# Two blocks' shift strips moved from the norm stage into the projection, with their stage weights loaded twice

## The reference

```python
sh, sc, gt = adaln(c, w_ada[l], b_ada[l])              # silu(c) @ w_ada + b_ada, in thirds
sh_c, sc_c, gt_c = adaln(c_ctx[None], w_ada[l], b_ada[l])
h_l = rmsnorm(x_l, norm_g[l]) * (1.0 + sc) + sh        # 512 x 2048
h_c = rmsnorm(x_c, norm_g[l]) * (1.0 + sc_c) + sh_c    # 256 x 2048
u_l = h_l @ w_in[l]                                    # the projection, 39 column tiles of 128
u_c = h_c @ w_in[l][:, OFF_KV:OFF_MLA_G]
```

## Time and profile before

| | |
|---|---|
| median of the runs | 901.35 us |
| the profiled execution: its own time | 901.99 us |
| its span, first to last instruction | 900.2 us |
| busy: PE, DVE, ACT, POOL | 98%, 77%, 47%, 22% |
| mean granted TensorE clock | 0.997 of full |
| stage A on PE | until 126.7 us |
| DMA queue of SP | 147.25 MB of 184.08 |

### The profile page before, as it was taken

How to read it: one execution, slowest core, us unless ns; L and a number is a source line. 1 busy time by engine, 2 the same in 40 slices (tenths; PEclk the granted TensorE clock), 3 DMA queues, 4 the chain that set the end, 5 groups by cost and what they waited for, 6 DMA issues and landing times.

```text
span 900.2 us, 12252 instructions
## 1 busy us (share of the span) xinstructions
PE 886.3 (98%) x4750; PEld 739.2 (82%) x4750; DVE 696.5 (77%) x860; ACT 426.2 (47%) x633; POOL 200.0 (22%) x167
## 2 busy tenths in 40 slices
PE   9999999999999999999999999999999999999996
PEld 5776688888888888888888888989898988888885
DVE  5555898789997699967787484778687787879796
ACT  4655467434335434333324332645454456645464
POOL 1222200310003100001002753100000200495641
PEclk9999999999999999999999999999999999999998
DMA  9999932235473453578874242865657535875754
GB/s 362 417 420 421 409 145 95 89 129 189 143 183 106 114 167 117 187 232 325 314 295 162 94 140 94 181 228 141 135 171 198 123 140 187 305 228 187 234 186 187
DMA packets 36885, 184.08 MB, mean 204 GB/s; under 512 B 4411, under 2 KB 5819, under 8 KB 26716
## 3 DMA queue, kind: packets, MB, share of 16 engines
q1 hardware_dynamic: 32528, 147.25, 44.4%
q0 software_dynamic: 3968, 35.65, 16.2%
q10 hardware_dynamic: 332, 0.40, 0.1%
HBM read 177.39 MB, written 37.75 MB: 239 GB/s over the span
## 4 chain that ended last, share of the span: by engine, by line
PE 90%; DMA 4%; DVE 3%; ACT 2%; issue 1%; SPq 0%; ACTq 0%; DVEq 0%
PE pp L2346 41%; PE pp L2376 17%; PE pp L2656 17%; PE pp L2261 4%; DMA ada_raw<-in_w_ada_dram 3%; PE pp L2237 3%; PE pp L2622 2%; PE pp L2267 1%; PE pp L2613 1%; PE pp L2614 1%; DMA ada_raw<-in_w_scale_dram 1%; DVE softmax_stats L1854 1%; DVE pt_lo L1869 0%; ACT U L1140 0%; PE pp L2445 0%
## 5 line engine op out<-in xcount | busy, mean ns | idle before, releaser
L2346 PE MATMUL pp<-h_hi,w_hi 128*128 128x512 f32 x544 | 213.0, 391 | 0.0
L2346 PE MATMUL pp<-h_hi,w_lo 128*128 128x512 f32 x544 | 211.8, 389 | 0.0
L2346 PE MATMUL pp<-h_lo,w_hi 128*128 128x512 f32 x544 | 211.8, 389 | 0.0
L1569 DVE TENSOR_TENSOR w_lo<-w_raw,w_hi 128x1024 fp32r<-128x1024 f32 x68 | 91.0, 1339 | 62.6 <-ACT w_hi L931 61.8
L931 ACT ACTIVATE w_hi<-w_raw 128x1024 fp32r<-128x1024 f32 x68 | 71.8, 1056 | 130.8 <-PE pp L2346 114.9
L2346 PEld LDWEIGHTS pp<-h_hi,w_lo 128*128 128x128 f32 x544 | 102.1, 188 | 21.5
L2346 PEld LDWEIGHTS pp<-h_hi,w_hi 128*128 128x128 f32 x544 | 102.2, 188 | 21.1 <-DVE w_lo L1569 0.3
L2346 PEld LDWEIGHTS pp<-h_lo,w_hi 128*128 128x128 f32 x544 | 102.2, 188 | 20.5
L2656 PE MATMUL pp<-wo_hi,side_hi 128*128 128x512 f32 x224 | 87.3, 390 | 0.1
L2656 PE MATMUL pp<-wo_hi,side_lo 128*128 128x512 f32 x224 | 87.2, 389 | 0.0
L2656 PE MATMUL pp<-wo_lo,side_hi 128*128 128x512 f32 x224 | 87.2, 389 | 0.0
(11 more groups left out here) (368 smaller groups left out, 1930.8 us busy)
## 6 DMA issues: line engine op xcount, KB each, us to landing
w_raw<-in_wb_dram SPq DMA_DIRECT2D x68, 512.0 KB, 3.8
ada_raw<-in_w_ada_dram SPq DMA_DIRECT2D x15, 2048.0 KB, 13.5
w_out_sums<-in_w_out_dram POOLq DMA_DIRECT2D x16, 1024.0 KB, 10.4
w_gate_raw<-in_w_gate_dram SPq DMA_DIRECT2D x16, 1024.0 KB, 7.4
wo_raw<-w_out_sums SPq DMA_DIRECT2D x16, 1024.0 KB, 5.0
wo_raw<-in_w_out_dram SPq DMA_DIRECT2D x12, 1024.0 KB, 5.0
wa_raw<-in_wa_dram SPq DMA_DIRECT2D x14, 288.0 KB, 8.3
UG<-in_xT_dram SPq DMA_DIRECT2D x7, 512.0 KB, 9.2
```

The costliest lines, as they stand in the source:

```text
L1569: eng.tensor_tensor(lane(wb_lo, n % KW), lane(wb_raw, n % KW), lane(wb_hi, n % 2), ALU.subtract).then_inc(wb_lo_done, 1)
L2346: mm = eng.matmul(ps[i][:], w, x, start=(kk == 0 and m == 0), stop=(kk == KT - 1 and m == 2))
```

## The change

The shifts of blocks 0 and 1 are no longer made in stage A. Their `w_ada` load becomes the seventeenth, `LATE = 16`, behind all others. `ada_vectors(LATE)` stands in the projection behind part 0 of chunk 0, its `combine` behind chunk 1, ACT's `late_shifts` in chunk 2. The projection takes its channel blocks in the order 2, 3, ..., 15, 0, 1 (`place_of`, `block_at`), so that the tokens of blocks 0 and 1, which need these shifts, are made last, in chunk 2. `wa_first` is gone: the two weight blocks are loaded a second time for `shifted(0)` and `shifted(1)`, which DVE does in chunk 2.

The sums over the partitions can then be made only behind chunk 3 (`shift_columns`), and ACT copies them out there. `ps[0]` and `ps[1]` of the stage are copied out without the bias; `first_shifts` adds it in place in chunk 4, and only then come the two `centre`s, once in chunk 1. The `neighbour_taps` of tiles 0 and 1 move from chunk 2 to chunks 5 and 6. The context's sum of squares, once behind the shift sums, stays in the stage.

```diff
-NEIGHBOURS = (2, 2, 8, 8, 10, 10, 18, 19, 26, 26, 30, 34)
+NEIGHBOURS = (5, 6, 8, 8, 10, 10, 18, 19, 26, 26, 30, 34)
-EARLY, LATE = 2, 13
+EARLY, LATE = 2, KT
+def block_at(p):
+    return (p + EARLY) % KT
...
@@ SP @@
             for j in range(2, KT):
-                if j == LATE:
-                    load_ada(LATE)
-                load_ada(block_of(j))
+                load_ada(j)
...
+            load_ada(LATE)
             eng.wait_ge(ada_mm, KT - 1)
             for n in range(KW):
                 load_b(n)
             load_decay(0)
             load_decay(1)
+            load_wa(KT)
             eng.wait_ge(scaled, 4)
             load_w3(0)
             eng.wait_ge(a_lo_done, 2 * KT)
             eng.wait_ge(csum_done, KT)
+            load_wa(KT + 1)
...
@@ ACT, stage A @@
-                if j + 2 == LATE:
-                    rows_out(LATE)
-                    late_shifts()
...
@@ ACT, new functions @@
+            def shift_columns():
+                eng.wait_ge(sum_mm, 4)
+                eng.activation(shift_cols[:], ps[7][:, 256:264], ACT.Copy).then_inc(root_done, 1)
+
+            def first_shifts():
+                eng.wait_ge(root_done, 4)
+                eng.wait_ge(evA_done, 5)
+                for i in range(2):
+                    eng.activation(conv_raw(i), conv_raw(i), ACT.Identity, bias=shift_cols[:, i:i + 1], scale=1.0).then_inc(shifted_in, 1)
+                for i in range(2):
+                    eng.wait_ge(shifted_in, 3 + i)
+                    centre(i)
...
@@ ACT, projection @@
             eng.wait_ge(sum_mm, 3)
-            eng.activation(shift_cols[:], ps[7][:, 256:264], ACT.Copy).then_inc(root_done, 1)
+            eng.activation(tmp[:, L:LK], ps[7][:, 0:256], ACT.Sqrt, bias=eps[:, 0:1], scale=1.0 / D).then_inc(root_done, 1)
...
-                eng.activation(conv_raw(i), ps[i][:], ACT.Identity, bias=shift_cols[:, i:i + 1], scale=1.0).then_inc(evA_done, 1)
+                eng.activation(conv_raw(i), ps[i][:], ACT.Copy).then_inc(evA_done, 1)
...
                 if n == 1:
                     tokens(12)
                     tokens(13)
-                    eng.wait_ge(evA_done, 2)
-                    for i in range(2):
-                        centre(i)
...
                 if n == 2:
+                    late_shifts()
                     tokens(14)
                     tokens(15)
...
+                if n == 3:
+                    shift_columns()
...
+                if n == 4:
+                    first_shifts()
...
                 if n % 4 == 3 and n not in (TF[0] + 3, TF[1] + 3):
                     evacuate(2 * (n // 4))
@@ DVE @@
-                if j + 2 == LATE:
-                    for k in range(EARLY):
-                        shifted(k)
...
                     tokens(14)
                     tokens(15)
-                    for i in range(2):
-                        neighbour_taps(i)
+                    for k in range(EARLY):
+                        shifted(k)
@@ PE @@
-                    if j + 2 == LATE and i == 3:
-                        eng.wait_ge(root_done, 2)
-                        ada_vectors(LATE)
...
-                    if j + 2 == LATE and i == 4:
-                        combine(LATE)
...
                         if i == 1:
-                            shift_columns()
+                            context_square_sums()
...
                 half_chunk(n, 0)
+                if n == 0:
+                    ada_vectors(LATE)
...
                 half_chunk(n, 1)
+                if n == 1:
+                    combine(LATE)
+                if n == 3:
+                    shift_columns()
```

More of the change, by code:

```diff
@@ L61, with place_of @@
 X_STEPS = (0, 2, 4, 5, 7, 8, 9, 10)
-EARLY, LATE = 2, 13
-def block_of(k):
-    return k + (k >= LATE)
+EARLY, LATE = 2, KT
 def shifts_of(k):
-    return (k + 1 if k >= LATE else LATE - 1 + k if k < EARLY else k - 1)
+    return (KT - 1 + k if k < EARLY else k - 1)
+def place_of(k):
+    return (k - EARLY) % KT
+def block_at(p):
+    return (p + EARLY) % KT
 CHUNKS = [(1, 0, 0), (1, 1, 0), (1, 0, 1), (1, 1, 1)] + [(u, b, c) for u, b in (
@@ L465, in load_x @@
                     eng.wait_ge(sq_done, 2 * p - 6)
[L466 to L467 removed]
+                a, n = (2 * p, 2) if p else (1, 1)
+                to = place_of(a) * L
+                eng.dma_start(UG[:, to:to + n * L], t["xT"][:, a * L:(a + n) * L]).then_inc(x_in[p % 4], 16)
             def load_c(p):
@@ L1227, in _ @@
                 if n == 0:
-                    eng.activation(tmp[:, L:LK], ps[7][:, 0:256], ACT.Sqrt, bias=eps[:, 0:1], scale=1.0 / D).then_inc(root_done, 1)
-                    for k in range(8, 12):
-                        tokens(k)
+                    tokens(8)
+                    tokens(9)
+                    rows_out(LATE)
+                    hidden_high()
+                    tokens(10)
+                    tokens(11)
                 if n == 1:
@@ L1449, in shifted @@
             def shifted(j):
-                w = wa_raw(j)
-                eng.wait_ge(wa_in[j % 2], 16 * (j // 2) + 16)
+                w, load = wa_raw(j), j + KT if j < EARLY else j
+                eng.wait_ge(wa_in[j % 2], 16 * (load // 2) + 16)
                 eng.wait_ge(mod_done, shifts_of(j))
@@ L2007, in _ @@
                 for i in range(12):
-                    if NEIGHBOURS[i] == n and n not in (2, 8, 18, 30, 34):
+                    if NEIGHBOURS[i] == n and n not in (5, 6, 8, 18, 30, 34):
                         neighbour_taps(i)
@@ L2039, in _ @@
                 for i in range(12):
-                    if NEIGHBOURS[i] == n and n in (18, 30, 34):
+                    if NEIGHBOURS[i] == n and n in (5, 6, 18, 30, 34):
                         neighbour_taps(i)
@@ L2226, in ada_vectors @@
                 if b:
-                    eng.wait_ge(mod_scale, b - (b > LATE))
+                    eng.wait_ge(mod_scale, b)
                 if b > EARLY:
-                    eng.wait_ge(mod_done, b - EARLY + (EARLY - 1) * (b > LATE))
+                    eng.wait_ge(mod_done, b - EARLY)
+                if b == LATE:
+                    eng.wait_ge(root_done, 3)
                 eng.wait_ge(ada_in[b % 3], 16 * (b // 3) + 16)
@@ L2272, in square_sums, with context_square_sums @@
                 eng.matmul(ps[7][:, 256:512], ones[:], rstd[:, r * LC:(r + 1) * LC], start=True, stop=True).then_inc(sum_mm, 1)
+            def context_square_sums():
+                eng.wait_ge(csum_done, KT)
+                eng.wait_ge(root_done, 2)
+                eng.matmul(ps[7][:, 0:256], ones[:], rstd_c[:], start=True, stop=True).then_inc(sum_mm, 1)
             def shift_columns():
                 eng.wait_ge(row_sums, KT)
-                eng.wait_ge(csum_done, KT)
-                eng.wait_ge(root_done, 2)
                 for i in range(8):
                     w = shift_x[:, i * P:(i + 1) * P] if i < 5 else shift_c[:, (i - 5) * P:(i - 4) * P]
-                    eng.matmul(ps[7][:, 256 + i:257 + i], w, ones[:, 0:1], start=True, stop=True)
-                eng.matmul(ps[7][:, 0:256], ones[:], rstd_c[:], start=True, stop=True).then_inc(sum_mm, 1)
+                    mm = eng.matmul(ps[7][:, 256 + i:257 + i], w, ones[:, 0:1], start=True, stop=True)
+                mm.then_inc(sum_mm, 1)
             def hidden(layer):
@@ L2322, in _ @@
                             eng.wait_ge(root_done, j - 10)
-                        ada_vectors(block_of(j + 1))
-                    if j + 2 == LATE and i == 3:
-                        eng.wait_ge(root_done, 2)
-                        ada_vectors(LATE)
+                        ada_vectors(j + 1)
                     if i == 1 and 0 < j < KT - 1:
-                        combine(block_of(j + 1))
-                    if j + 2 == LATE and i == 4:
-                        combine(LATE)
+                        combine(j + 1)
                     if i == 1 and j in (10, 11):
@@ L2782, in layout @@
             + [tile(o_pool + i * P) for i in range(4)] + [tile(o_pg + i * P) for i in range(4)])
+    rest = [np.roll(x, -EARLY * P, axis=0) for x in rest]
     wa = np.concatenate(first, axis=1).reshape(KT, P, A_TILES * P - DR)
@@ L2786, in layout @@
     late = np.stack([w_ada[:, :P].reshape(KT, P, P), w_ada[:, P:2 * P].reshape(KT, P, P)], axis=2)[:, :, None]
-    blocks = np.concatenate([ss[:, :, EARLY:LATE], late, ss[:, :, LATE:]], axis=2)
+    blocks = np.concatenate([ss[:, :, EARLY:], late], axis=2)
     gate = w_ada[:, 2 * D:]
```

44 lines of the change are left out of this document (20 added, 24 removed).

## The result

| | before | after |
|---|---|---|
| median of the runs, us | 901.35 (901.06 to 901.38, 5 runs) | 909.16 (908.00 to 909.63, 5 runs) |
| ratio | | 1.0084, 95% interval [1.0069, 1.0098] |
| profiled execution, time (span), us | 901.99 (900.2) | 909.16 (907.4) |
| PE / DVE / ACT busy, us | 886.3 / 696.5 / 426.2 | 889.1 / 695.2 / 427.4 |

The change costs 7.8 us in the medians and 7.2 in the profiled executions. I had forecast 4.9 and a range that ended at 908.0: the direction was right, the size was not.

A forecast was written before the change was run, and what follows sets the result against it. The prediction took PE's matmuls, 90% of the chain, to bound the kernel. Its terms, -3.0 + 4.2 - 0.2 + 1.0 + 1.0 + 1.0 + 0.9 = +4.9, gave a median of 906.25 us, range 902.8 to 908.0.

The forecast's parts named there:

- Terms 1 to 4: Stage A to chunk 4: earlier projection start -3.0, PE work added there +4.2, a lost wait -0.2, new wait +1.0.
- term 1: Projection start: PE arrives 4.7 us earlier but waits 1.7 for the first bank, so chunk 0 starts 3.0 earlier.
- term 4: Ahead of chunk 4: PE waits for ACT's copy out of ps[0], held up by the shift columns; +1.0 us.
- a start of chunk 0 before 123: Sign at the projection's start that the forecast is wrong, DVE not being the limit; forecast start 123.7.
- term 3: Projection's first 108 matmuls: 0.25 us lost to a wait for DVE goes, as PE gets there later; -0.2 us.
- The rival that took stage A for bound by its bytes: Stage A is DMA-bound, its end moves by the load's 5.0 us; sum -1.0, 900.35 us; chance 0.06.
- Term 6: Taps' relay, third spectrum: DVE's neighbour_taps(0), priced at 1.45 us, makes the sums late; PE loses +1.0 us.
- terms 5 to 7: Relay of taps between DVE, ACT and PE, chunks 4 to 8: PE waits before three spectra, +1.0, +1.0, +0.9.
- Rival 1: Taps' relay: ACT's and DVE's pauses absorb the added work, terms 5 to 7 shrink to 0.3; 903.7 us; chance 0.20.

The follow-up runs named there:

- e7_norm_first: e1_evac_first with DVE's norms and ACT's copies of the first two projection banks ahead of scale and token steps 6 and 7; 905.49 us.
- e1_evac_first: The kernel after, with ACT's copy of the shift columns put behind the evacuation of ps[0] instead of ahead of it; 906.91 us.
- e12_after_again: The kernel after, unchanged, run again; 909.03 us.
- e10_small_pool_sums: e1_evac_first with GpSimd's additions in the second to fourth taps step cut to 8 columns; 904.59 us.
- e5_taps_in_gaps: e1_evac_first with DVE's neighbour operations moved: tile 0's to its wait for chunk 6's weights, tile 1's into its waits for tap_hi; 903.50 us.
- e6_relay_only: The kernel before, with only the centres and neighbour operations of tiles 0 and 1 moved behind the first, and the second and third, taps steps; 904.55 us.
- e11_columns_between_parts: The kernel after, with PE's sixteen one-column matmuls ahead of the second part of chunk 3 instead of behind it; 906.77 us.
- e9_shifts_behind_weights: e1_evac_first, e5_taps_in_gaps and e7_norm_first together, with ACT's shift additions and centres behind chunk 6's w_hi and neighbour operations one step later; 901.17 us.

## Why the prediction was wrong, and where it was right

- **Terms 1 to 4 were right as sums**: -3.07 for -3.0, and +4.93 for 4.2 - 0.2 + 1.0. PE's last matmul of stage A ends at 121.32 (122.24 without the offset), then comes the wait of 1.41 that ACT's `UG` ends; I had 122.0 and 1.7. The reading behind term 1 (the projection is entered when DVE and ACT have the bank ready, so only 3.0 of the 4.7 us that PE saves count) was shown by e7_norm_first, that behind term 4 by e1_evac_first. I had named a start of chunk 0 before 123 as a sign that term 1 is wrong, and it starts at 122.73; but the wait is there, and in e1_evac_first and e12_after_again, with the same wait, the start is at 123.10 and 123.22. The sign stood only 0.7 below the forecast of 123.7, and executions are offset by up to 0.9. Among the small parts, the strips' matmuls took 2.2 for 2.5, the wait 0.85 for 1.0, and term 3 did not come: the 96 matmuls took 0.2 longer, not 0.2 less. The rival that took stage A for bound by its bytes is out: the start moved by 3.07, not by the load's 5.0, and what PE waited for was ACT and DVE.
- **Term 6 was mis-sized, and this is the step that failed**: "`neighbour_taps(0)` behind it takes 144.18 - 142.73 = 1.45". It took 3.4, and PE lost 2.74 us by this term instead of 1.0. I had priced the pair by rows from chunk 2, where GpSimd does nothing: it is idle for the 40.09 us ahead of 157.34. In steps from one `tap_lo` to the next the relay became 1.90, 2.29 and 1.37 us longer (9.42, 9.48 and 9.93 us), where I had 2.5, 0.55 (1.45 less 0.9) and 1.45; less the 1.5 that PE had to spare at the end, +4.06 for +2.9. The second step is 1.7 too small. The first is 0.6 too large: 0.4 of it were ACT's copies and centres ahead of chunk 5's `w_hi`, but there DVE still waits 1.29 for PE, and the first `tap_lo` is as late as the first taps, 2.8. That the pair's length beside GpSimd is what cost it is shown by e10_small_pool_sums and e5_taps_in_gaps, and by e6_relay_only in the kernel before. The hint had been among my own rows: `w_lo` took 1.63 at 165.76. I used its length as time that could be given back and did not ask why it was long.
- **A term was missing**: the fall of the clock. Of the +1.86 in the profiled execution 1.68 is the clock's (4.57 against 2.89 in e1_evac_first). I had found the wait (term 4) and priced it as idle time alone. e1_evac_first and e11_columns_between_parts, which take only the wait away, are 2.2 and 2.3 us faster than the kernel after: the wait's own 0.85 and, in the median, the clock's share.
- **The range was too narrow for its own bounds.** 4.5 for terms 5 to 7 with 1.9 for term 4 gives 908.75, above the 908.0 where it ended; the relay's +4.06 lies within that 4.5. The sum given for its lower end is wrong too: 0.8 for terms 5 to 7 makes +2.8 and 904.15, not 903.7.
- **Rival 1, that the relay holds, was wrong in this kernel**, though e9_shifts_behind_weights shows that it can be had. I had held against it that the idle 1.20 ahead of each `tap_lo` is a latency and not room. It is room for a DVE operation that does not need what ACT is rounding: in e5_taps_in_gaps one of 0.75 stands in it each time, and 0.41 and 0.34 of idle time are left.

The six numbers add up: -0.92 - 3.07 + 4.93 + 1.86 + 4.06 + 0.32 = 7.18, for 7.2 measured in the span. Of the 2.3 us by which the forecast missed this span (905.1 for 907.4), 1.7 are term 6 and 1.9 the slow part 0, less 0.9 of offset and 0.4 of small terms. The offset hid part of the miss; that is luck.

## What to carry to other kernels

When an operation is moved, price it by a row from the place where it will run, not from where it ran: ask what GpSimd does there if it reads two inputs from SBUF. A row that is longer than its kind, as a `w_lo` of 1.63 among ones of 1.23, is the trace's way of telling that. And a wait of under a microsecond, 0.85 here, behind a stretch of one-column matmuls can cost more than itself.
